# A three-sub-layer decoder block on eight cores: weight loads tied to TensorE's progress, both steps of the inverse roots on GpSimd, own-row sums placed later

## The chip, the cores and the metric

One Trainium2 chip, 8 cores. The same program runs on all eight, each on its own 2,048 rows of the sequence (2 batches of 8,192 rows, four cores to a batch); no core talks to another. The metric is the time of the slowest core in device microseconds, the median of several runs. The names of the engines in the rows: PE is TensorE (matmul), PEld its weight load, DVE VectorE, ACT ScalarE, POOL GpSimd, SP the sync engine; a q behind a name is that engine's instruction queue, which issues transfers too.

## The reference, cut to what matters

With D = 1024, D_FF = 2816 and nine modulation vectors per batch (shift, scale and gate for each of three sub-layers, from `silu(c) @ w_ada + b_ada`):

```
h = modulate(rms_norm(x), sh1, sc1);  x = x + 0.5 * gt1 * swiglu(h, ffn1)
h = modulate(rms_norm(x), sh2, sc2);  x = x + gt2 * hybrid_mixer(h)
h = modulate(rms_norm(x), sh3, sc3);  x = x + 0.5 * gt3 * swiglu(h, ffn2)
rms_norm(x)      = x / sqrt(mean(x*x) + 1e-6) * g
modulate(h,s,c)  = h * (1 + c) + s
swiglu(h)        = (silu(h @ w_gate) * (h @ w_up)) @ w_down
```

The mixer projects h to queries, keys, values and convolution inputs, runs dilated causal attention over the last 2,048 positions and a short convolution, merges both by gates and projects again. Because of the attention's reach every core also needs h of the 2,048 rows ahead of its own (its halo), and computes the first feed-forward part for them itself.

## The kernel before, in words

**Stages.** A core's 16 tiles of 128 rows are taken in four groups `tg` of 512 rows. The order of the work is: first feed-forward over the halo rows (pass 0, from `xh`), the same over the own rows (pass 1, from `xo`), the mixer, the second feed-forward over the own rows. The rows live in `xbuf` (tensor `A`, f32), the transposed and normed input of the matmuls in `hT` (tensor `B`), the weights in two slots of tensor `Dw`, hidden values in `E` (and parts of `C`).

**Feed-forward (`ffn`).** D_FF is cut into six `PIECES` of 4, 4, 2, 4, 4, 4 column blocks of 128. For each piece and each of the four row groups there is a unit: `gu` does the gate and up projections (for each block j eight matmuls into bank j%2, a Silu by ACT, eight matmuls into bank 2+j%2, a product by DVE into `hid`), and `down` the down projection (8 groups of `nj` matmuls, each followed by a DVE addition into `xbuf`). Two passes of six pieces give pieces p = 0 to 11; the second feed-forward has p = 0 to 5. Piece p uses slot p%2. The weights of piece p+2 are loaded while piece p+1 runs: `load_gu` has eight transfers (four gate, four up), `load_d` one transfer for each block, and 20 us of planned time later DVE multiplies the down weights by the gate row (`scale_task`). The transfers are issued by POOL and convert f32 to bf16.

**The plan.** The program's order is written by a planner at build time. `P.t` is a planned time that advances with every matmul (0.213 us for 512 columns). Side work is written as generators on lanes (`Lanes`); `yield x` asks to be resumed when `P.t` is x later, and `L.tick()`, called after every group of matmuls (every 1.7 planned us in `gu`, 0.85 in `down`), resumes what is due. So the plan says beside which matmul an instruction is written. At run time there is no clock: each engine works through its own queue in order, and an instruction waits only for the semaphores of what it reads, overwrites, or follows on its DMA channel. `quiet()` makes the load generators pause while `P.t < L.hold`; `head` of `Norm` sets `L.hold` 8 planned us past every norm it writes. `L.finish(task)` writes all that is left of a task at once; `ffn` calls it before the first unit of a piece (gate and up loads) and before its first `down`.

**The norms (`Norm`, `norm_pe`).** For a row group: four sums of squares on ACT (`sumsq`, into `ssb`), then `roots`: a multiply and add on DVE, `(mean + eps)`, 128 x 4 values, then a power of -0.5 on POOL; then `scaled`, four multiplications of 128 x 1024 on POOL, each followed by a DMA transpose issued by SP into the transposed buffer; after `settle` planned us the `rest`: eight DVE modulations of 128 x 512 in three portions. `norm_pe` (only in the opening) transposes on PE instead.

**Where the two passes meet.** When the last piece of pass 0 (piece 5) is through `down` for row group tg, `post(u)` starts `n2[0, tg]`, the mixer's norm of the halo rows (delay 1.5, settle 15, in buffers `xn_a` of `C`). Behind its scaling, `mid` loads the own rows of that group over the halo rows (`load_x(xo_d, tg)`, 2 MB) and starts `n1[1, tg]`, the own rows' norm for the first feed-forward, 11 planned us later and with settle 11. It must be finished before piece 6 reaches that row group, about 51 planned us behind `post`. `put` stores the halo rows' h (`h2s`, 1 MB).

```
            def mid():
                load_x(xo_d, tg)
                n1[1, tg] = Norm("n1", 11.0, tg, xn_b, 2, 0, 8)
```

**Where the second feed-forward opens.** `head3` loads piece 0 and computes the last part of the mixer's output; `spawn_n3` starts norms `n3`. `late2` is called behind `gu` of the third unit and spawns both loads of piece 1, because its slot held the mixer's `mTs` and `tab`:

```
            if i == 2 and late is not None:
                late(load)
```

The opening of the first feed-forward (`opening`) has a like place: the loads of piece 1 are spawned in the middle of the fourth unit's `gu`, behind `gates()`.

Of the kernel before, what the change touches and what calls it, by code (L numbers as in the profile page):

```python
# [11 lines left out]

EPS = 1e-6
D = 1024
KC = 8
# [256 lines left out]
def build_nc():  # L272
# [27 lines left out]
    P = Prog()  # L300
# [35 lines left out]
    def mm(out, lhsT, rhs, start, stop):  # L336
        cols_ = 1
        for _, c in list(rhs.ap)[1:]:
            cols_ *= c
        P.t += max(cols_ / 2400.0, 0.027)  # L340
        return P.op("pe", "matmul", out, lhsT=lhsT, rhs=rhs, start=start, stop=stop)

# [22 lines left out]

    def wide_load(dst, src, chan):
        return P.op("pool", "dma_start", out=dst, in_=src.rearrange("(k p) n -> p k n", p=128), chan=chan)

# [7 lines left out]

    def load_gu(w, s, j0, nj):

        n = nj * 128
        for q in range(4):  # L380
            for j, nm in ((0, "wg"), (1, "wu")):
                yield from quiet()
                wide_load(SV[s][j][:, 2 * q:2 * q + 2, 0:n], w[j][q * 256:(q + 1) * 256, j0 * 128:j0 * 128 + n], (nm, s, q))
                yield 3.4

    def load_d(w, s, j0, nj):
        for j in range(nj):
            yield from quiet()
            wide_load(SV[s][2][:, j:j + 1, :], w[2][(j0 + j) * 128:(j0 + j + 1) * 128, :], ("wd", s, j))
            yield 3.4  # L390
# [93 lines left out]
    def roots(tg, ss):  # L484
        c0 = ss * NT + 4 * tg
        ts(out=rstd[:, c0:c0 + 4], in0=ssb[:, c0:c0 + 4], scalar1=1.0 / D, scalar2=EPS, op0=ALU.mult, op1=ALU.add)
        tt("pool", out=rstd[:, c0:c0 + 4], in0=rstd[:, c0:c0 + 4], in1=mhalf[:], op=ALU.pow)
# [16 lines left out]
    class Norm:  # L504
# [7 lines left out]
        def head(self, lane, tg, xns, ss, acol, scol, mid, post, dst, hurry, settle, before):  # L512
# [8 lines left out]
            roots(tg, ss)  # L521
            L.hold = max(L.hold, P.t + 8.0)
            for i in range(4):
# [82 lines left out]
    def ffn(passes, pre, post, head=None, flip=0, gates=None, each=None, late=None):  # L606
# [12 lines left out]
        def load(p, what):  # L619
# [4 lines left out]
            if what == 0:  # L624
                ups[p] = L.spawn("up", load_gu(w, s, j0, nj))
                if p == 0:
                    L.finish(ups[p])
            else:
                now = load_d(w, s, j0, nj)
                if p == 0:  # L630
# [74 lines left out]
    P.op("pool", "dma_start", out=brow, in_=bada_d[2 * D:3 * D].rearrange("(o n) -> o n", o=1), chan="brow")  # L705
    run(load_d(f1, 0, *PIECES[0]))
    n1[0, 0] = None
# [27 lines left out]
    def post(u):  # L735
        tg = u.tg
        tk = slice(tg * 512, (tg + 1) * 512)
        if u.pi == 0:
# [4 lines left out]
            def mid():  # L743
                load_x(xo_d, tg)
                n1[1, tg] = Norm("n1", 11.0, tg, xn_b, 2, 0, 8)

# [496 lines left out]
```

How the kernel before makes its waits and increments, by code:

```python
                def body(engine, ops_e=ops_e, e=e):  # L207
                    for op in ops_e:
                        for k, v in op.waits:
                            engine.wait_ge(sems[k], v)
                        if op.fn is None:
                            continue
                        name, a, kw = op.fn
                        ins = getattr(engine, name)(*a, **kw)
                        if op.chan is not None:
                            ins.then_inc(sems[("c", op.chan)], 16)
                        elif op.needs_inc:
                            ins.then_inc(sems[("e", e)], 1)
```

## Time and profile before

| | us |
|---|---|
| median of 3 runs, slowest core | 2414.03 (2408.94 to 2418.44) |
| the profiled execution, its own time | 2409.29 |
| span of its slowest core (core 3) | 2407.7 |
| PE busy in that span | 2270.4 (94%) |
| DVE, ACT, POOL busy | 1098.9, 609.0, 513.8 |
| spans of the eight cores | 2389.7 to 2407.7 |

The profile is of one execution and one core. Its time is 1.6 us more than the span of the core. Every instruction stands under the line of the helper that issues it (L214), so instructions are told apart by their tiles: `C<-A` with 128x1024 elements on ACT is a sum of squares, `rstd` the roots, `C<-A,rstd` the scaling, `B<-C` or `C<-C` on SP a transpose, `B<-B,cols` a modulation, `E<-ps,E` the product of gate and up, `A<-ps,A` the addition behind a down projection, `Dw<-ffn_w_...` a weight load. The figure in brackets at the end of a timeline row is the engine's idle time ahead of the instruction, and what ended it.

### The profile page before, as it was taken

How to read it: one execution, taken by the hardware profiler on the slowest of the kernel's cores; microseconds unless marked ns; L12 is line 12 of the kernel's file. 1: busy time of each engine (PE TensorE's matmuls, PEld its weight loads, DVE VectorE, ACT ScalarE, POOL GpSimd, SP SyncE). 2: the span in 40 equal slices, each digit the busy share in tenths (PEclk: the TensorE clock that was granted, in tenths of full speed). 3: DMA queues.
4: the chain of work that ended last, by engine and by line, in shares of the span. 5: the costliest groups of instructions: out<-in, count | busy, mean ns of one | idle time of the engine just before them, and what ended most of it. 6: DMA issues, size and time to landing. Idle time of an engine off the chain costs nothing.

```text
span 2407.7 us, 32141 instructions; the slowest of 8 cores (2389.7 to 2407.7 us)
## 1 busy us (share of the span) xinstructions
PE 2270.4 (94%) x11524; PEld 1051.0 (44%) x11524; DVE 1098.9 (46%) x1876; ACT 609.0 (25%) x1044; POOL 513.8 (21%) x612
## 2 busy tenths in 40 slices
PE   3999999987999999989999999999999979999999
PEld 1444444433444444434444544444444434434444
DVE  1264544455534444454444444666434434454444
ACT  2501111132010111245676665211122211111110
POOL 2300201134201220133544535210011221020100
PEclk8999999999999999999999999999999989999999
DMA  9932713359536651474242535831111442150302
GB/s 184 169 47 36 100 23 53 53 145 205 85 48 87 88 93 48 101 145 59 33 47 37 56 40 78 117 37 26 49 48 49 105 80 27 14 83 10 53 36 105
DMA packets 260586, 174.48 MB, mean 72 GB/s; under 512 B 172112, under 2 KB 239824, under 8 KB 258512
## 3 DMA queue, kind: packets, MB, share of 16 engines
q0 software_dynamic: 152336, 135.82, 34.9%
q1 hardware_dynamic: 108096, 36.62, 8.0%
q8 instruction: 96, 1.57, 0.3%
q14 instruction: 58, 0.48, 0.1%
HBM read 221.56 MB, written 20.97 MB: 101 GB/s over the span
## 4 chain that ended last, share of the span: by engine, by line
PE 84%; DMA 6%; ACT 2%; issue 2%; DVE 2%; POOL 2%; SPq 1%; another core or an unknown queue 0%; DVEq 0%; ACTq 0%; POOLq 0%
PE ps L214 84%; DMA Dw<-ffn_w_gate 2%; DMA C<-C 1%; SPq L214 1%; ACT Dw L214 1%; ACT C L214 1%; DMA A<-xo 1%; POOL C L214 1%; DMA B<-C 1%; DVE A L214 1%; DMA B<-B 1%; DMA B<-Dw 0%; POOL rstd L214 0%; ACT A L214 0%; DMA A<-Dw 0%
## 5 line engine op out<-in xcount | busy, mean ns | idle before, releaser
L214 PE MATMUL ps<-B,Dw 128*128 128x512 bf16 x6144 | 1391.8, 384 | 40.5 <-DVE E L214 20.2
L214 PEld LDWEIGHTS ps<-B,Dw 128*128 128x128 bf16 x6144 | 600.7, 99 | 759.1 <-issue 83.4
L214 DVE TENSOR_TENSOR A<-ps,A 128x512 f32<-128x512 f32 (+2 forms) x768 | 480.5, 644 | 184.1 <-PE ps L214 177.4
L214 ACT ACTIVATE E<-ps 128x512 f32<-128x512 f32 x296 | 176.2, 596 | 1316.6 <-PE ps L214 1276.3
L214 PE MATMUL ps<-Dw,E 128*128 128x512 bf16 x2048 | 467.8, 380 | 29.1 <-DVE A L214 27.1
L214 DVE TENSOR_TENSOR E<-ps,E 128x512 bf16<-128x512 f32 (+1 forms) x288 | 199.0, 691 | 649.1 <-PE ps L214 642.0
L214 PEld LDWEIGHTS ps<-Dw,E 128*128 128x128 bf16 x2048 | 195.4, 98 | 285.0 <-issue 62.4
L214 ACT ACTIVATE Dw<-ps 128x512 bf16<-128x512 f32 (+2 forms) x280 | 163.3, 588 | 259.9 <-PE ps L214 256.7
L214 POOL DMA_DIRECT2D Dw<-ffn_w_gate x70 | 51.6, 737 | 451.6 <-PE ps L214 451.6
L214 POOL TENSOR_TENSOR Dw<-Dw,E 128x512 bf16<-128x512 bf16 x96 | 110.7, 1153 | 142.9 <-ACT Dw L214 142.7
L214 PE MATMUL ps<-B,C 128*128 128x512 bf16 x512 | 121.0, 379 | 0.0
L214 DVE CAST Dw<-ps 128x512 bf16<-128x512 f32 x72 | 48.1, 668 | 136.2 <-PE ps L214 131.8
L214 ACT ACTIVATE Dw<-ps,cols 128x512 f32<-128x512 f32 x120 | 80.7, 673 | 60.9 <-PE ps L214 60.3
L214 PE MATMUL ps<-A,Dw 128*128 128x512 bf16 x384 | 93.3, 379 | 0.0
L214 POOL DMA_DIRECT2D Dw<-w_in x60 | 55.3, 929 | 173.1 <-PE ps L214 163.2
L214 PE MATMUL ps<-C,Dw 128*128 128x512 bf16 (+1 forms) x384 | 81.1, 357 | 5.7 <-DVE Dw L214 5.7
L214 DVE SCALAR_TENSOR_TENSOR Dw<-Dw,ps 128x512 f32<-128x512 f32 x64 | 43.9, 687 | 92.9 <-PE ps L214 87.4
L214 PE MATMUL ps<-Dw,A 128*128 128x128 bf16 x768 | 72.0, 221 | 13.1 <-DVE A L214 10.7
L214 PEld LDWEIGHTS ps<-Dw,A 128*128 128x128 bf16 x768 | 56.7, 98 | 47.6 <-issue 25.3
L214 ACT ACTIVATE Dw<-Dw 128x512 f32<-128x512 f32 x120 | 74.3, 619 | 11.3 <-ACT Dw L214 0.4
L214 PE MATMUL ps<-Dw,ones_s 128*128 128x512 bf16 (+1 forms) x216 | 72.3, 335 | 5.0 <-ACT Dw L214 5.0
L214 PEld LDWEIGHTS ps<-B,C 128*128 128x128 bf16 x512 | 50.1, 98 | 60.4
(88 smaller groups left out, 1086.8 us busy)
## 6 DMA issues: line engine op xcount, KB each, us to landing
Dw<-ffn_w_down POOLq DMA_DIRECT2D x66, 256.0 KB, 10.5
Dw<-w_in POOLq DMA_DIRECT2D x60, 256.0 KB, 5.8
Dw<-ffn_w_gate POOLq DMA_DIRECT2D x56, 256.0 KB, 8.6
Dw<-ffn_w_up POOLq DMA_DIRECT2D x56, 256.0 KB, 10.5
C<-w_ada POOLq DMA_DIRECT2D x24, 512.0 KB, 8.1
A<-xo POOLq DMA_DIRECT2D x4, 2048.0 KB, 11.3
x1s<-A POOLq DMA_DIRECT2D x4, 2048.0 KB, 7.2
A<-x1s POOLq DMA_DIRECT2D x4, 2048.0 KB, 8.7
```

Of the source, the lines that this page charges most:

```text
L214: ins = getattr(engine, name)(*a, **kw)
```

## The change

Four edits. Every `wide_load` of `load_gu` and `load_d` with `paced` true gets `P.last`, the matmul written last at that point of the plan, as a further dependence: POOL's queue then waits for that matmul's semaphore before it issues the load. `paced` is true for p > 0, so for 16 of the 18 pieces. `HOLD` is 14 where 8 stood. The first step of `roots` moves from DVE to POOL, where the second is. The own rows' norm starts 20 planned us behind `mid` where 11 stood, and its modulations follow its roots after 16 where 11 stood.

```diff
--- before.py
+++ after.py
@@ -11,6 +11,7 @@
 ALU = mybir.AluOpType
 
 EPS = 1e-6
+HOLD = 14.0
 D = 1024
 KC = 8
 DFF = 2816
@@ -338,7 +339,8 @@
         for _, c in list(rhs.ap)[1:]:
             cols_ *= c
         P.t += max(cols_ / 2400.0, 0.027)
-        return P.op("pe", "matmul", out, lhsT=lhsT, rhs=rhs, start=start, stop=stop)
+        P.last = P.op("pe", "matmul", out, lhsT=lhsT, rhs=rhs, start=start, stop=stop)
+        return P.last
 
     def turn(out, in_, chan):
         return P.op("sp", "dma_start_transpose", out=out, in_=in_, chan=chan)
@@ -363,8 +365,8 @@
     def load_x(src_d, tg):
         P.op("pool", "dma_start", out=xbuf[:, 4 * tg:4 * tg + 4, :], in_=src_d[:, 4 * tg:4 * tg + 4, :], chan=("xg", tg))
 
-    def wide_load(dst, src, chan):
-        return P.op("pool", "dma_start", out=dst, in_=src.rearrange("(k p) n -> p k n", p=128), chan=chan)
+    def wide_load(dst, src, chan, after=()):
+        return P.op("pool", "dma_start", out=dst, in_=src.rearrange("(k p) n -> p k n", p=128), chan=chan, after=after)
 
     slots = [Dw[:, s * 12288:(s + 1) * 12288] for s in range(2)]
 
@@ -374,19 +376,23 @@
                 b[:, 8192:12288].rearrange("p (j n) -> p j n", j=4))
     SV = [slot_views(s) for s in range(2)]
 
-    def load_gu(w, s, j0, nj):
+    def here(paced):
+
+        return (P.last,) if paced else ()
+
+    def load_gu(w, s, j0, nj, paced=True):
 
         n = nj * 128
         for q in range(4):
             for j, nm in ((0, "wg"), (1, "wu")):
                 yield from quiet()
-                wide_load(SV[s][j][:, 2 * q:2 * q + 2, 0:n], w[j][q * 256:(q + 1) * 256, j0 * 128:j0 * 128 + n], (nm, s, q))
+                wide_load(SV[s][j][:, 2 * q:2 * q + 2, 0:n], w[j][q * 256:(q + 1) * 256, j0 * 128:j0 * 128 + n], (nm, s, q), here(paced))
                 yield 3.4
 
-    def load_d(w, s, j0, nj):
+    def load_d(w, s, j0, nj, paced=True):
         for j in range(nj):
             yield from quiet()
-            wide_load(SV[s][2][:, j:j + 1, :], w[2][(j0 + j) * 128:(j0 + j + 1) * 128, :], ("wd", s, j))
+            wide_load(SV[s][2][:, j:j + 1, :], w[2][(j0 + j) * 128:(j0 + j + 1) * 128, :], ("wd", s, j), here(paced))
             yield 3.4
 
     def run(gen):
@@ -483,7 +489,7 @@
 
     def roots(tg, ss):
         c0 = ss * NT + 4 * tg
-        ts(out=rstd[:, c0:c0 + 4], in0=ssb[:, c0:c0 + 4], scalar1=1.0 / D, scalar2=EPS, op0=ALU.mult, op1=ALU.add)
+        ts("pool", out=rstd[:, c0:c0 + 4], in0=ssb[:, c0:c0 + 4], scalar1=1.0 / D, scalar2=EPS, op0=ALU.mult, op1=ALU.add)
         tt("pool", out=rstd[:, c0:c0 + 4], in0=rstd[:, c0:c0 + 4], in1=mhalf[:], op=ALU.pow)
 
     def scaled(tg, xns, ss, i, other):
@@ -519,7 +525,7 @@
             if before is not None:
                 before()
             roots(tg, ss)
-            L.hold = max(L.hold, P.t + 8.0)
+            L.hold = max(L.hold, P.t + HOLD)
             for i in range(4):
                 scaled(tg, xns, ss, i, "dve" if hurry else "pool")
                 for ap, k0, k1 in xns[i].parts:
@@ -622,11 +628,11 @@
             pi, q, w, gi, j0, nj = seq[p]
             s = (p + flip) % 2
             if what == 0:
-                ups[p] = L.spawn("up", load_gu(w, s, j0, nj))
+                ups[p] = L.spawn("up", load_gu(w, s, j0, nj, p > 0))
                 if p == 0:
                     L.finish(ups[p])
             else:
-                now = load_d(w, s, j0, nj)
+                now = load_d(w, s, j0, nj, p > 0)
                 if p == 0:
                     run(now)
 
@@ -703,7 +709,7 @@
     load_x(xh_d, 3)
     wide_load(blk[2], wada_d[:, 2 * D:3 * D], "blk2")
     P.op("pool", "dma_start", out=brow, in_=bada_d[2 * D:3 * D].rearrange("(o n) -> o n", o=1), chan="brow")
-    run(load_d(f1, 0, *PIECES[0]))
+    run(load_d(f1, 0, *PIECES[0], False))
     n1[0, 0] = None
     n1[0, 1] = L.spawn("n1", norm_pe(1, xn_b, 0, 0, 8), 6.5)
     n1[0, 2] = L.spawn("n1", norm_pe(2, xn_b, 0, 0, 8))
@@ -742,7 +748,7 @@
 
             def mid():
                 load_x(xo_d, tg)
-                n1[1, tg] = Norm("n1", 11.0, tg, xn_b, 2, 0, 8)
+                n1[1, tg] = Norm("n1", 20.0, tg, xn_b, 2, 0, 8, settle=16.0)
 
             def put(m):
                 P.op("pool", "dma_start", out=h2s_d[:, :, tk], in_=hss[tg % 2], chan=("h2s", tg))
```

## Rows read from the trace of the kernel before

**Rows 1.** The page: the span, and which core it is.
```profile
span 2407.7 us, 32141 instructions; the slowest of 8 cores (2389.7 to 2407.7 us)
```

**Rows 2.** What PE waited for, whole span: total us, times, longest.
```profile
PE ps L214 <- DVE A L214: 37.8, 23, 16.6
...
PE ps L214 <- DVE E L214: 20.9, 7, 5.7
...
PE ps L214 <- ACT E L214: 7.8, 4, 2.4
```

**Rows 3.** Two stretches: us; busy PE, PEld, DVE, ACT, POOL; clock; DMA share; GB/s.
```profile
490.20:610.60 120.40, 92.79 (x386) 38.91 (x385) 69.24 (x121) 38.15 (x72) 52.85 (x56) 0.90 0.82 184
1939.10:1978.50 39.40, 22.81 (x97) 9.78 (x96) 10.65 (x20) 2.39 (x4) 3.54 (x6) 0.78 0.61 97
```

**Rows 4.** Timeline, PE, two starts of `down` that nothing disturbs.
```profile
1978.54 7.07 PE L214 MATMUL ps<-Dw,E 128*128 128x512 bf16 x32
...
1999.26 7.07 PE L214 MATMUL ps<-Dw,E 128*128 128x512 bf16 x32
```

**Rows 5.** Timeline, where the passes meet: load, sums, and PE's two pauses.
```profile
476.67 0.69 DVE L214 TENSOR_TENSOR A<-ps,A 128x512 f32<-128x512 f32 x1 [0.17 <-PE ps L214]
...
489.74 0.62 POOL L214 DMA_DIRECT2D A<-xo  x1 [0.58 <-POOL C L214]
...
501.68 1.06 ACT L214 ACTIVATE C<-A 128x1024 bf16<-128x1024 f32 x1 [12.28 <-DMA A<-xo]
...
506.56 1.89 PE L214 MATMUL ps<-B,Dw 128*128 128x512 bf16 x8 [2.38 <-ACT E L214]
...
507.36 5.23 DVE L214 TENSOR_SCALAR C<-C,cols 128x512 bf16<-128x512 bf16 x6
...
513.33 6.88 PE L214 MATMUL ps<-B,Dw 128*128 128x512 bf16 x19 [4.88 <-DVE E L214]
```

**Rows 6.** What DVE waited for from 478 to 604 us.
```profile
DVE rstd L214 <- ACT C L214: 35.9, 5, 8.8
```

**Rows 7.** Transfers, us to landing: transposes at 486, 491, 522, 1944; own rows.
```profile
C<-C SPq DMA_TRANSPOSE x1, 3.3
...
C<-C SPq DMA_TRANSPOSE x1, 12.3
...
C<-C SPq DMA_TRANSPOSE x1, 13.9
...
B<-C SPq DMA_TRANSPOSE x1, 17.2
...
A<-xo POOLq DMA_DIRECT2D x1, 2048.0 KB, 11.8
```

**Rows 8.** Timeline of 1930 to 1962: transposes, first and last of twelve loads, PE's pause.
```profile
1934.90 18.93 SPq L214 DMA_TRANSPOSE B<-C  x4
...
1934.64 0.78 POOL L214 DMA_DIRECT2D Dw<-ffn_w_gate  x1
...
1941.85 0.79 POOL L214 DMA_DIRECT2D Dw<-ffn_w_up  x1
...
1961.88 1.87 PE L214 MATMUL ps<-Dw,E 128*128 128x512 bf16 x4 [16.59 <-DVE A L214]
```

**Rows 9.** Weight transfers, us to landing: near-alone at 734.5, 736.3; burst from 275.
```profile
Dw<-ffn_w_gate POOLq DMA_DIRECT2D x1, 256.0 KB, 3.9
...
Dw<-ffn_w_up POOLq DMA_DIRECT2D x1, 256.0 KB, 4.6
...
Dw<-ffn_w_gate POOLq DMA_DIRECT2D x4, 256.0 KB, 11.5
```

**Rows 10.** The tile `rstd`: ns min/median/max, first and last start.
```profile
L214 DVE TENSOR_SCALAR rstd<-ssb x20: 157/170/172, 17.3 to 1928.7; 128x4 f32<-128x4 f32 x20
L214 POOL TENSOR_TENSOR rstd<-rstd,mhalf x20: 1006/1032/1377, 17.6 to 1929.0; 128x4 f32<-128x4 f32 x20
```

**Rows 11.** Timeline, DVE: modulations with POOL not scaling beside them.
```profile
1033.05 1.05 DVE L214 TENSOR_SCALAR B<-B,cols 128x512 bf16<-128x512 bf16 x3
```

## The prediction, made before the changed kernel had run

> **What bounds the kernel now.** I read the page first, then PE's waits, then a table of stretches, then the timeline of the two worst. The span is 2407.7 us [rows 1] and PE computes in 94% of it, so what can be had is PE's idle time and its time at half clock. Three groups of waits matter, on the halves of work that DVE and ACT hand back: 37.8, 20.9 and 7.8 us [rows 2]. The table of stretches says where most of it lies [rows 3]. From 490.2 to 610.6, where halo pass and own pass meet, PE is busy for 92.79 of 120.40 us and its mean granted clock is 0.90. From 1939.1 to 1978.5, at the opening of the second feed-forward, it is busy for 22.81 of 39.40 us at 0.78. An undisturbed unit of four blocks takes 1999.26 - 1978.54 = 20.72 us [rows 4]. The first stretch is four units, 82.9 us, so its excess is 37.5 us: 27.6 idle, and 9.9 in which PE ran at 1.2 instead of 2.4 GHz after its pauses. The second is one unit and has 18.7 us too much: 16.6 idle and 2.1 of slow clock. Together 56.2 us: all that this change aims at.
>
> **Why PE pauses there.** In the first stretch the own rows' load is issued at 489.74 and takes 11.8 us [rows 5, 7]. The sums that need it are written about 9 planned us earlier than it lands, so ACT stands for 12.28 us until 501.68, with Silus behind the sums; PE pauses for 2.38 us for a Silu. DVE has the first step of the roots in its queue and stands with ACT: 35.9 us in five waits [rows 6]. When it is free it owes six modulations (5.23 us), and PE waits another 4.88 us for the product behind them [rows 5]. The pattern comes four times. The second stretch is a collision. Four transposes stand in SP's queue from 1934.90; POOL, whose slot is free, issues twelve weight loads from 1934.64 to 1941.85 although the plan writes them some 55 us into the stage, behind the third unit's gate and up work; the last transpose takes 17.2 us where an unhindered one takes 3.3, DVE waits for it, and PE stands for 16.59 us [rows 7, 8].
>
> **Part 1, the wait on the matmul.** In the second stretch it moves all twelve loads behind the third unit's gate and up work. The transposes then meet no weight traffic: issued to about 1940, landed 3.3 us later, with the modulations due at about 1942. I book 17.5 of the 18.7 us, about 1 us being left for a transpose a little late. What queues behind a waiting load is POOL's later work; it is written later in the plan too and mostly hangs on PE's results of that moment, so I cost that at nothing. It is covered as long as POOL has slack (513.8 us busy of 2407.7).
>
> What becomes late is the end of each piece's loads. Eight gate and up loads at 3.4 planned us need 27 us; a normal piece has 82 from their spawning to its first unit, the two-block piece some 44, and a weight load lands in 3.9 to 4.6 us with little beside it [rows 9]. So the steady pieces lose nothing. Two places have little slack. In the opening, spawning and first use are 27.3 planned us apart: the last gate load goes out 5.1 us and the last up load 1.7 us before the unit, whose matmuls ask for them 1.3 and 3.0 us into it; landing fits within half a us, and I take 0. In the second feed-forward the distance is 20.5 us, six loads fit, and `finish` writes the last gate and up load with a wait on the last matmul ahead of the unit. PE does six matmuls of 0.216 us (1.3 us) and stands until the gate load lands: 0.15 to wake POOL (my estimate, from the gap of 0.17 us behind PE in [rows 5]) + 3.9 + 0.1 - 1.3 = 2.9 us. The up load lands before it is asked for. Bounds: 0, if a row is late anyway, and 11.5 - 1.3 = 10.2 us at a burst's landing [rows 9]; 2.9 is nearest, as by then only those two are in flight.
>
> **Part 2, the own rows' sums 9 us later.** Counted from `post` at 476.6, where the group's last additions run [rows 5], the load goes out at 13.1 us and lands at 25; the sums are now due at the tick of 25.6 planned, 25.9 real. ACT no longer stands, and PE's waits for Silus go. The own modulations are due at 46 behind their `post`, needed at 51, so the pass does not wait.
>
> **Part 3, the first root step on POOL.** Twenty times DVE loses 0.17 us and one hand-over; POOL gains an operation [rows 10]. POOL's only 128 x 4 row is the power, 1.03 us, which bounds it from above; below it is 0.1. It is nearer in kind to a multiply than to a power, so I take 0.3, less the hand-over saved: 0 on the path. The ends are -0.1 and +0.9 us for each of some seven places where PE hangs on the roots (three in the opening, four where the mixer opens): -1 to +6 in all. What it brings is that DVE no longer stands for ACT's sums (35.9 us in this stretch [rows 6]).
>
> **Part 4, HOLD 14.** It closes more of the meeting stretch to loads. With roots at 5.1 and 29.0 planned us behind each `post`, 20.5 apart, what stays open for piece 7's loads is one slot at 64, two at 84 to 90, and all from 104 behind the first `post`. Each lane has its last gate or up load out by 118, for a `finish` at 133. No cost; the transposes there meet one or two loads in place of six.
>
> **What is late next in the meeting stretch.** The fourth transpose of the halo norm is issued just behind the own rows' load and takes 12.3 us, and 13.9 with the store of h beside it [rows 7]. Nothing in the change moves that. It lands at 25.8 (first group) or 27.3 behind `post`, while the modulations are due at 20.7. DVE then does six (2.1 us at 0.35 [rows 11]) and the product (0.69): 28.6 or 30.1, against 29.4 when PE wants that bank. Then come eight own modulations before the next unit may end its first group, about 1.6 us late in all. So about 0 + 3 x 1.6 = 5 us stay, and 2 us for half clock behind them: 37.5 - 7 = 30 us gained. If the modulations went at 0.87 us (six in 5.23 [rows 5]), 14 of them would add 7 us to each of three groups, 21 in all.
>
> Here a rule bears on the rows. A transpose took 3.3 us alone and 12.3 behind a load of 2 MB, so I let it wait for the load. The Trainium skill, DMA: Bandwidth & Descriptors, section Queues, rings and completion order, has it that each DMA engine goes round-robin over the queue rows it has work for, one packet at a time, so that SP's transpose would share with POOL's load and not stand behind it. By that rule the sum would be that of the clean rival below; the rows do not agree with it in size.
>
> **The sum.** -30 (meeting) - 17.5 (opening of the second feed-forward) + 2.9 (late pair) + 0 (roots) = -44.6. On the profiled execution's 2409.3 us that gives 2364.7, on the median of 2414.0, which is 4.7 higher, 2369.4. I forecast 2368.
>
> **The rivals.** *Both stretches clean.* If transposes shared the engines fairly with the load beside them, the fourth would take about twice 3.3 us, land at 20, and nothing would stay of the 37.5 and 18.7: -56.2 + 2.9 = -53.3, 2361 us. Against it: 12.3 and 17.2 us are four and five times 3.3 [rows 7]; for it: at 1940 the twelve loads that the change moves away are all there is beside the transposes. This is where the skill's round-robin rule would lead. Chance 0.20.
>
> *The meeting stretch stays bad.* The late transpose and 16 modulations in a row keep DVE behind, at 0.87 us each: 21 us more than booked, so only 9 us are gained there: -9 - 17.5 + 2.9 = -23.6, 2390 us. For it: the fourth transpose there takes 13.9 us today [rows 7]. Against: POOL scales at another time. Chance 0.19.
>
> *Loads late at every piece: slower.* If the 16 paced pieces had no slack, through a hold or a wait of POOL's queue behind something slow, each would end like the late pair. At 2.9 us each, 46 us, that eats the gain; beyond it the change loses. With the eight loads out together at 11.5 us, less 1.3, it is 10.2 x 16 = 163 us: 2414 - 47 + 163 = 2530. Against it stand 82 us of distance for 27 us of issue. Chance 0.05.
>
> *The wait binds nowhere*, because the slots free at the planned time anyway: then the collision at 1940 stays and only parts 2 and 3 count, about half of the first stretch's 27.6 idle us: 2400. The twelve loads in 7.2 us, against 20.5 planned [rows 8], say otherwise. Chance 0.04.
>
> **How the numbers follow.** My case has 0.52. Range 2353 to 2392: the low end is the clean case with 8 us for chip and run, the high end the bad meeting stretch; outside lie slower, not binding and the tails. A measurement of this kernel can tell about 0.5% (12 us) from no change. Faster by more: 0.52 + 0.20 + 0.19, less a little, 0.90; within: 0.05; slower: 0.05.
>
> **What the profile of after would show.** Right: the twelve loads of piece 1 of the second feed-forward 3.4 us apart behind the third unit, the pause of 16.59 us gone, one of about 3 us before the fifth unit, waiting for a `ffn_w_gate` or `ffn_w_up` load; DVE with no wait for the sums; ACT's wait for `A<-xo` near 0; PE's clock at 1.00 around 600; the stretch of four units near 90 us in place of 120.4. Wrong: pauses of PE for weight loads in several pieces; product waits of 3 us or more in the meeting stretch (then DVE's C<-C waits are the cause); POOL's step above 1 us.

## The result, and the profile after

The changed kernel took 2396.25 us, the median of five runs, beside 2410.51 for the kernel before, the median of five too. The ratio is 0.9927, with a 95% interval of 0.9907 to 0.9948, and is taken from the means of the executions, 2394.8 and 2412.4 us. (Executions in which the cores of one die ran at a much lower granted clock than the other's, such as those of 2610.8 and 2708.5 us among the five, are left out of it and of every ratio and mean below.) So the kernel is faster by 0.73%, 14 us by the medians and 17.5 by these means, and not by the 45 that were forecast; 2396.25 lies above the range of 2353 to 2392.

The page, and the waits of PE over the whole span, for core 4, the slowest of the profiled execution. They answer to [rows 1] and [rows 2]; the columns of a wait are total us, times, longest.

```profile
span 2391.3 us, 32217 instructions; the slowest of 8 cores (2364.4 to 2391.3 us)
```

```profile
PE ps L215 <- DVE A L215: 21.0, 23, 3.3
PE ps L215 <- DVE E L215: 16.5, 5, 12.2
...
PE ps L215 <- DMA Dw<-ffn_w_gate: 8.5, 3, 4.4
PE ps L215 <- DVE B L215: 7.7, 6, 5.8
```

PE's wait for additions (`DVE A`) fell from 37.8 to 21.0 us and its longest from 16.6 to 3.3: the pause at the opening of the second feed-forward is gone. The waits for Silus (`ACT E`, 7.8 before) have left the list. But the product wait (`DVE E`) now has a single piece of 12.2 us where the longest was 5.7, and `DVE B`, the wait for the modulations of the own rows, is new.

Two measures carry the rest. **By units:** on every core I read the starts of `down` from PE's timeline and take the distance from one to the next, which is 20.7 us undisturbed [rows 4]. The meeting stretch is the eight units around the meeting, 165.8 us undisturbed; the four of them that the prediction spoke of are the third to the sixth. The opening of the second feed-forward is taken as its first four units, 82.9 us undisturbed. Means over the eight cores of one profiled execution:

| unit of the meeting stretch | 1st, 2nd | 3rd | 4th | 5th | 6th | 7th, 8th | all eight | opening of 2nd FF |
|---|---|---|---|---|---|---|---|---|
| before | 20.7 | 29.0 | 28.0 | 31.4 | 30.0 | 20.7 | 201.2 | 99.7 |
| after | 20.7 | 20.7 | 28.2 | 22.6 | 34.6 | 20.7 | 189.0 | 90.5 |

So 12.2 us came from the meeting stretch and 9.2 from the opening of the second feed-forward. The time up to the first of these marks grew from 448.1 to 450.7 us, and what lies between the two places changed by -1.0. The sum is -19.8, and so is the difference of the mean spans of the eight cores (2399.8 and 2380.0). The metric takes the slowest core of each execution, and that one gained less, 16.4 us here (2407.7 to 2391.3).

**By middle core:** for the small differences between experiments I take the median of the eight spans of a timed execution, its mean over the executions, and its distance from the same number of the kernel before on the same chip. Its standard error is 1 to 4 us (e9 and e10 have a single execution each, so none). The stretches, by contrast, are read from one profiled execution of each kernel.

The table of stretches for core 4: the four units of the meeting, a part of them, then the third unit of the second feed-forward. The first row answers to the first of [rows 3]; columns as there.

```profile
493.30:607.90 114.60, 92.12 (x386) 38.58 (x385) 59.68 (x108) 38.36 (x72) 50.50 (x56) 0.87 0.87 186
...
565.00:601.50 36.50, 18.52 (x79) 7.67 (x76) 9.75 (x21) 5.46 (x9) 9.36 (x12) 0.75 1.06 190
1977.10:2003.90 26.80, 22.43 (x98) 9.68 (x97) 8.30 (x12) 2.39 (x4) 7.70 (x12) 0.94 0.83 120
```

On this core the four units still take 114.6 us: 22.5 idle, and, against 82.9, another 9.2 at the lower clock. Of the idle time, 18.0 us are in the 36.5 us from 565.0, where PE is busy for 18.5 and the busy share of the DMA engines is 1.06, beside 0.87 for the four units.

What DVE and ACT waited for from 470 to 640 us, core 4. This answers to [rows 6].

```profile
DVE C L215 <- DMA C<-C: 30.3, 4, 17.2
DVE B L215 <- DMA B<-C: 10.2, 3, 8.2
...
ACT C L215 <- DMA B<-C: 20.1, 3, 16.3
```

DVE's wait for sums (35.9 us before) is gone, and ACT no longer waits for `A<-xo`. Both now wait for transposes: DVE for those of the halo rows (`C<-C`) and of the own rows (`B<-C`), ACT for transposes that still read the buffers into which the next own-row sums write.

The timeline of core 4 at the fourth row group, chosen lines. It answers to [rows 5].

```profile
563.68 0.62 POOL L215 DMA_DIRECT2D A<-xo  x1 [0.58 <-POOL C L215]
564.30 0.93 POOL L215 DMA_DIRECT2D h2s<-C  x1
...
572.66 23.34 SPq L215 DMA_TRANSPOSE B<-C  x4
...
575.29 0.78 POOL L215 DMA_DIRECT2D Dw<-ffn_w_up  x1 [4.01 <-PE ps L215]
...
579.43 0.56 POOL L215 DMA_DIRECT2D Dw<-ffn_w_down  x1
...
589.30 2.03 DVE L215 TENSOR_SCALAR C<-C,cols 128x512 bf16<-128x512 bf16 x6 [17.23 <-DMA C<-C]
...
592.08 3.57 PE L215 MATMUL ps<-B,Dw 128*128 128x512 bf16 x8 [12.17 <-DVE E L215]
...
593.49 1.06 ACT L215 ACTIVATE C<-A 128x1024 bf16<-128x1024 f32 x1 [16.34 <-DMA B<-C]
...
600.79 1.06 DVE L215 TENSOR_SCALAR B<-B,cols 128x512 bf16<-128x512 bf16 x3 [8.21 <-DMA B<-C]
...
601.46 2.04 PE L215 MATMUL ps<-B,Dw 128*128 128x512 bf16 x4 [5.81 <-DVE B L215]
```

Own rows, store of h and four weight loads are issued within 16 us. DVE stands for 17.23 us in front of the halo norm's modulations, with PE's product queued behind them, and PE loses 12.17 us. The six modulations then take 2.03 us. Next the own rows' modulations are late too, for 5.81 us more. The transfers of that moment, us from issue to landing: the fourth halo transpose, issued at 565.30, the first own transpose, issued at 572.66, and for comparison three of the first group (490 to 492). They answer to [rows 7]:

```profile
C<-C SPq DMA_TRANSPOSE x1, 23.7
...
B<-C SPq DMA_TRANSPOSE x1, 20.7
...
C<-C SPq DMA_TRANSPOSE x3, 3.2
```

Core 4 is one of two cores on which the long pause stands in front of the product. The mean over the eight cores is 6.0 us of waits for the product (`DVE E`; single pieces above 10 us only on cores 3 and 4) and 10.2 us for the own modulations (`DVE B`; 11.0 to 12.9 us at once on cores 1, 2, 5 and 6).

Even the issue of a transpose stood still. In the chain of waits of the same core, SP's queue holds two single pieces of 7.21 and 11.54 us, the issues of these same two transposes, where an undisturbed one has 1.23:

```profile
559.93 1.23 SPq L215
...
565.30 7.21 SPq L215
...
572.66 11.54 SPq L215
```

At the opening of the second feed-forward, core 4 (timeline; answers to [rows 8]):

```profile
1976.11 0.79 POOL L215 DMA_DIRECT2D Dw<-ffn_w_gate  x1 [44.93 <-PE ps L215]
...
1979.56 0.71 POOL L215 DMA_DIRECT2D Dw<-ffn_w_up  x1 [2.10 <-PE ps L215]
...
1995.10 0.72 POOL L215 DMA_DIRECT2D Dw<-ffn_w_gate  x1 [0.99 <-PE ps L215]
1995.82 0.72 POOL L215 DMA_DIRECT2D Dw<-ffn_w_up  x1
...
2000.20 2.29 PE L215 MATMUL ps<-B,Dw 128*128 128x512 bf16 x5 [4.37 <-DMA Dw<-ffn_w_gate]
```

The twelve loads start at 1976.11, behind the matmuls they are tied to: the gate and up loads 3.45 us apart, with the four down loads beside the first four of them. Before, all twelve stood within 7.2 us, beside the transposes. The last gate and up load go out together at 1995.10 and 1995.82, and PE waits 4.37 us for the first of them.

The step that moved to POOL (answers to [rows 10]; ns min/median/max):

```profile
L215 POOL TENSOR_SCALAR rstd<-ssb x20: 189/196/484, 17.7 to 1925.2; 128x4 f32<-128x4 f32 x20
```

### The profile page after: what moved, and what is told of

Its sections match the earlier page's. It is cut to its first block, busy times and chain, and to the rows that moved or that the text cites. A ratio compares the mean times of both kernels' runs of the same rounds, so it can differ in the third digit from the quotient of the medians.

```text
span 2391.3 us, 32217 instructions; the slowest of 8 cores (2364.4 to 2391.3 us)
## 1 busy us (share of the span) xinstructions
PE 2268.7 (95%) x11524; PEld 1049.9 (44%) x11524; DVE 1089.2 (46%) x1856; ACT 609.2 (25%) x1044; POOL 518.5 (22%) x632
## 4 chain that ended last, share of the span: by engine, by line
PE 86%; DMA 4%; SPq 2%; ACT 2%; issue 2%; POOL 2%; DVE 1%; another core or an unknown queue 0%; DVEq 0%; ACTq 0%; POOLq 0%
PE ps L215 86%; SPq L215 2%; DMA Dw<-ffn_w_up 2%; ACT Dw L215 1%; DMA B<-C 1%; POOL C L215 1%; DVE A L215 1%; ACT C L215 1%; DMA B<-Dw 1%; POOL rstd L215 0%; ACT A L215 0%; DMA A<-Dw 0%; POOL Dw L215 0%; DVE Dw L215 0%; DMA Dw<-ffn_w_gate 0%
## 5 line engine op out<-in xcount | busy, mean ns | idle before, releaser
L215 POOL DMA_DIRECT2D Dw<-ffn_w_up x70 | 50.4, 719 | 162.1 <-PE ps L215 161.9
L215 PE MATMUL ps<-Dw,A 128*128 128x128 bf16 x768 | 72.0, 221 | 13.1 <-DVE A L215 12.3
L215 ACT ACTIVATE Dw<-Dw 128x512 f32<-128x512 f32 x120 | 74.3, 619 | 11.6 <-ACT Dw L215 0.8
## 6 DMA issues: line engine op xcount, KB each, us to landing
A<-xo POOLq DMA_DIRECT2D x4, 2048.0 KB, 11.3
```

What stands on the lines that cost most here:

```text
L215: ins = getattr(engine, name)(*a, **kw)
```

## The experiments

Each is the changed kernel with the edit shown, unless it says otherwise. In the first expectations "six units" and "a unit less" go by the marks as I counted them then; measured is always the eight-unit stretch defined above.

### Which part did what

**e1: the own rows' norm back to its old place.**

```diff
-                n1[1, tg] = Norm("n1", 20.0, tg, xn_b, 2, 0, 8, settle=16.0)
+                n1[1, tg] = Norm("n1", 11.0, tg, xn_b, 2, 0, 8)
```

> The changed kernel with the own rows' norm back at 11 planned us behind the load and a settle of 11; wait, hold of 14 and roots on POOL stay. Over the eight cores the meeting stretch (six units, from the second down of piece 4's last unit on) took a mean of 201.2 us before and 189.0 changed; undisturbed it is 165.8 less a unit. Theory A (the later own norm put its four transposes behind the next group's 2 MB load and store, where SP, ACT and DVE stand in turn, and that costs most of what did not come): the waits of ACT for a transpose B<-C and the double digit pauses of PE go, the early wait for the own rows' load comes back at about 12 us of ACT per group but costs PE only some 2 us each, and the stretch gets shorter than 189, the kernel 5 to 10 us faster than the change. Theory B (the later norm is what brought the gain in that stretch): it goes back towards 201 and the kernel to about 2400 to 2405.

Measured: ratio 0.9936 (0.9892 to 0.998); meeting stretch 198.9, middle core -12.4 us. The waits of core 4, 470 to 650 us:

```profile
PE ps L215 <- DVE A L215: 21.5, 4, 9.3
...
ACT C L215 <- DMA A<-xo: 61.0, 4, 17.0
```

ACT stands for the own rows again, up to 17.0 us at a time. The later place is worth some 10 us of the stretch (198.9 beside 189.0), and 7 by the middle core (-12.4 beside the -19.5 of e13 below).

**e4: the wait alone** (HOLD 8, roots on DVE, own norm early).

```diff
-HOLD = 14.0
+HOLD = 8.0
-        ts("pool", out=rstd[:, c0:c0 + 4], in0=ssb[:, c0:c0 + 4], ...
+        ts(out=rstd[:, c0:c0 + 4], in0=ssb[:, c0:c0 + 4], ...
-                n1[1, tg] = Norm("n1", 20.0, tg, xn_b, 2, 0, 8, settle=16.0)
+                n1[1, tg] = Norm("n1", 11.0, tg, xn_b, 2, 0, 8)
```

> The kernel before with the wait on the matmul alone: hold of 8, roots as before, own norm as before. The wait by itself should remove the pause of 16.6 us at the opening of the second feed-forward and bring the pause for the late pair (5 to 6 us on each core of the changed kernel, with 2 us of slow clock): the five downs there 91.4 us in place of 101.6. If that is all it does, about -10 us, 2400, and the meeting stretch stays at 201 us. If spacing the weight loads also helps the meeting stretch, that gets shorter by up to 5 us; if the wait harms it (loads now pushed into the transposes of the last groups), it gets longer.

Measured: ratio 0.9944 (0.99 to 0.9988), middle core -10.9 us. Cores 4 to 7 of its profile give 201.3 for the meeting stretch, as before the change, and 90.3 for the opening of the second feed-forward. The wait does its work at the second place and none at the first.

**e5: all but the wait.**

```diff
     def here(paced):
-        return (P.last,) if paced else ()
+        return ()
```

> The changed kernel without the wait on the matmul; hold 14, roots on POOL and later own norm stay. The pause at the opening of the second feed-forward comes back (16 us, five downs about 100 us in place of 90.4) and the pause for the late pair goes. In the meeting stretch theory W says POOL runs ahead of the hold only where its queue is free: piece 7's loads stand behind roots that wait for ACT, so they go out at about the planned time anyway and the stretch stays near 189; if the wait matters there, it is above 195. Kernel about 2405.

Measured: ratio 0.9978 (0.9941 to 1.0014), middle core -6.3 us. The meeting stretch is 188.9, as with the wait. The opening of the second feed-forward is 97.0, with cores from 87.4 to 104.7; on core 6 the old pause is there (waits, 1880 to 2050 us):

```profile
PE ps L215 <- DVE A L215: 19.0, 1, 19.0
...
DVE B L215 <- DMA B<-C: 19.0, 1, 19.0
```

The two halves of the change add up within the error: -10.9 for the wait and -6.3 for the rest make -17.2, where e13 below has -19.5 for both.

**e2: HOLD back to 8.**

```diff
-HOLD = 14.0
+HOLD = 8.0
```

> The changed kernel with a hold of 8 in place of 14. Theory W (weight loads beside the transposes cost the fourth group's pause): more of piece 7's loads now go out between the norms, so the meeting stretch is longer than 189, about 195 to 200, the kernel about 2403. My booking in the prediction (the hold costs and gains nothing): 189 and 2396.

Measured: ratio 0.9956 (0.9913 to 0.9999), meeting stretch 202.2, middle core -11.8. The worst core, 0, from 470 to 660 us:

```profile
PE ps L215 <- DVE B L215: 33.4, 4, 31.9
...
DVE B L215 <- DMA B<-C: 34.3, 2, 33.2
```

With HOLD at 8 the fifth unit takes 36.5 us on average (22.6 with 14) and the whole gain of the later norm is lost. HOLD 14, which I had booked at nothing, is thus worth 13 us of the stretch (8 by the middle core) once the own norm is late. Each alone is worth next to nothing. Beside the wait alone (-10.9), the later norm with HOLD at 8 has -11.8 (e2), and HOLD 14 with the early norm has -12.4 (e1).

**e3 and e14: the first root step back on DVE**, on two chips.

```diff
-        ts("pool", out=rstd[:, c0:c0 + 4], in0=ssb[:, c0:c0 + 4], ...
+        ts(out=rstd[:, c0:c0 + 4], in0=ssb[:, c0:c0 + 4], ...
```

> The changed kernel with the first step of the roots back on DVE. With the own sums written later, ACT seldom stands, so DVE's root step should wait little. If the move to POOL still matters, DVE's waits for ACT's sums come back with more than 5 us in the meeting stretch and it grows by 3 us or more; if the later sums alone did it, the stretch stays at 189 +- 2.

> e3 once more (first root step back on DVE). If POOL's root step costs time where the passes meet (POOL's queue then stands at the sums with the transfers behind it, or one more POOL instruction shifts the loads against the transposes), the stretch is again near 182 and under that of e13 by 5 us or more. If it was luck, the two are within 3 us.

Measured: 0.9935 (0.989 to 0.9979) and 0.9922 (0.9881 to 0.9963); middle core -21.8 and -22.9; meeting stretch 182.4 and 195.2. The 12.8 us between two profiled executions of one kernel are a warning about single profiles, and so about every stretch here that rests on one. The timed runs say that the step's engine makes no difference that shows; if any, DVE is the better by 2 or 3 us.

**e13: the changed kernel once more**, on the chip and beside the runs of e14 and e15, no edit.

> The changed kernel as it is, once more, on the chip of the next two. The meeting stretch was 189.0 us in its first execution and 190.2 in e7, which is the same there. If that is its level, 187 to 192 again, with a pause of 10 us or more on half of the cores; if the 182.5 of e3 was the luck of one execution, this can come out at 183 too.

Measured: 0.9937 (0.9909 to 0.9964), middle core -19.5, meeting stretch 187.7.

### What keeps the meeting stretch long

**e8: no weight loads there.** The gate, up and down loads of piece 7 wait until the last own norm is through.

```diff
+        def behind_norms(gen):
+            while not ((1, 3) in n1 and n1[1, 3].main.done):
+                yield 1.0
+            yield from gen
...
-                ups[p] = L.spawn("up", load_gu(w, s, j0, nj, p > 0))
+                gen = load_gu(w, s, j0, nj, p > 0)
+                if gates is not None and p == 7:
+                    gen = behind_norms(gen)
+                ups[p] = L.spawn("up", gen)
...
+                if gates is not None and p == 7:
+                    now = behind_norms(now)
```

> The changed kernel, with the eight gate and up loads and the four down loads of piece 7 held back until the last own norm's roots are written, so no weight load goes out while the passes meet. The meeting stretch is now read as eight units, from the down of piece 4's second to last unit to that of piece 6's last, 165.8 us undisturbed, 201.2 before, 189.0 changed (mean of eight cores). Theory W (the eight loads let in at 64 and at 84 to 90 planned us stretch the fourth group's transposes to 20 us and more): the double digit pause of the fourth group goes on all cores, the stretch falls to about 176. Theory X (the 2 MB load and the 1 MB store do it): no more than 3 us of difference, and one core or another still has a pause above 10 us.

Measured: ratio 0.9896 (0.9832 to 0.9961), middle core -30.5 us (-19.5 for the changed kernel in e13), meeting stretch 180.6. The sixth unit fell from 34.6 to 23.5 us; the fourth stayed at 27.7. The waits of core 2, the worst in the stretch:

```profile
PE ps L215 <- DVE E L215: 5.2, 1, 5.2
...
DVE C L215 <- DMA C<-C: 23.7, 4, 10.7
```

On core 4 the fourth halo transpose still takes 18.8 us to land (23.7 with the weight loads), but the first own transpose 11.3 (20.7), and PE's waits for the own modulations fall from 10.2 to 1.9 us for a core. So weight loads like the four at 575 to 579 are what makes pauses of 12 us out of shorter ones. The bill at the other end is 1.4 us in the eighth unit (22.1 us); that the loads now come close to their use there is my reading, not shown by a row.

**e9: a quarter of the own rows.** Only one of each group's four tiles is loaded, 0.5 MB in place of 2, so the rest of the own rows is not computed from its input.

```diff
-                load_x(xo_d, tg)
+                P.op("pool", "dma_start", out=xbuf[:, 4 * tg:4 * tg + 1, :], in_=xo_d[:, 4 * tg:4 * tg + 1, :], chan=("xg", tg))
```

> The changed kernel with only the first of the four tiles of each group's own rows loaded (0.5 MB in place of 2; the other three groups of rows keep what the halo pass left, so three quarters of the own rows are not the reference's). Theory X: the fourth transpose of each halo norm lands in about 5 us in place of 12 to 14, DVE's waits for C<-C (19.6 us a core) and B<-C (11.6 us) fall under 5 us each, the meeting stretch to about 170 to 174 us. Theory W: both waits stay in the fourth group, the stretch stays above 182.

In its single execution the meeting stretch is 172.5 us; the fourth unit is down to 23.1 and the sixth to 21.7, weight loads and all. DVE, core 2:

```profile
DVE C L215 <- DMA C<-C: 0.9, 2, 0.5
```

The own rows' load is the larger part of it: without three quarters of its bytes, neither the store of h nor the weight loads do much harm. Its middle core is -38.5 us.

**e6: the own rows' load 4.5 planned us later,** so that the fourth transpose of the halo norm goes first.

```diff
-                load_x(xo_d, tg)
+                def later():
+                    load_x(xo_d, tg)
+                    yield 0.0
+                L.spawn("xo", later(), 4.5)
```

> The changed kernel, with the own rows' load written 4.5 planned us later, so that on POOL it comes behind the previous group's own norm and all eight transposes of a group are issued before it. Theory A (transposes standing behind the 2 MB load and the 1 MB store are the cause): DVE's waits for C<-C and B<-C (17.2 and 8.2 us at worst on one core) and SP's issues of 7 to 11 us mostly go; what comes is a wait of ACT for the own rows' load of about 5 us per group, with little slack, 1 to 2 us of PE each; meeting stretch about 178 to 183 us, kernel about 8 us faster than the change. Rival (the weight loads let in at 64 and 84 planned us are the cause): no difference, the worst pause of PE stays in the fourth group.

Measured: ratio 0.9892 (0.9825 to 0.996), but middle core -19.3, like the changed kernel; meeting stretch 194.7. DVE's waits for the halo transposes went from 19.6 us for a core to 4.2, and those for the own transposes from 11.6 to 33.8. Core 6, 470 to 660 us:

```profile
PE ps L215 <- DVE B L215: 41.6, 3, 22.4
...
DVE B L215 <- DMA B<-C: 55.3, 3, 27.0
```

The wait moved from one norm to the other.

**e10: the own rows in four tiles,** 4 planned us apart, each with a wait on a matmul.

```diff
-                load_x(xo_d, tg)
+                def tiles():
+                    for i in range(4):
+                        n = 4 * tg + i
+                        P.op("pool", "dma_start", out=xbuf[:, n:n + 1, :], in_=xo_d[:, n:n + 1, :], chan=("xo", i), after=(P.last,))
+                        yield 4.0
+                L.spawn("xo", tiles())
```

> The changed kernel, with each group's own rows loaded by four transfers of 512 KB, 4 planned us apart and each with a wait on the matmul beside it, in place of one of 2 MB. The same bytes, spread over 12 us more. Theory X: a transpose now finds at most one tile ahead of it, some 3 us, so it lands in 4 to 8 us; DVE's waits for transposes fall by half or more, the stretch to about 176 to 180, the kernel about 8 us faster than the change; the sums find their tiles in time (last tile out at 12, landed by 17, due at 20). If it is the number of bytes in the stretch that counts and not how they are bunched, nothing changes (within 3 us).

A single execution, so no ratio. Meeting stretch 192.6; a single unit took up to 52 us, and DVE's waits for own transposes were 24.9 us for a core (11.6 in the changed kernel). Spreading a transfer over the transposes is no better than having it in one piece; the gain of 8 us that I expected is not there.

### The late pair, and both repairs

**e7: the loads of piece 1 of the second feed-forward spawned one unit earlier.**

```diff
-            if i == 2 and late is not None:
+            if i == 1 and late is not None:
```

> The changed kernel, with the loads of piece 1 of the second feed-forward spawned one unit earlier (behind the second unit's gate and up work in place of the third's). All eight gate and up loads are then out 27 planned us later with some 14 to spare, and they still start 10 us or more after the last transposes. The pause of 4.4 to 5.9 us for a ffn_w_gate load and the 2 us of slow clock behind it go: five downs take 83 to 85 us in place of 91.4, the kernel about 7 us faster than the change. If the pause is only replaced by another wait of DVE for transposes, it is no faster.

Measured: ratio 0.9881 (0.9804 to 0.9958), middle core -23.6; the four units took 83.4 us, 0.5 above undisturbed. The late pair has time, and the transposes, which stand close before, don't suffer. On core 3 one wait of PE is left from 1880 to 2050 us; the longest on any core is 3.6 us (core 7), and none is for a weight load:

```profile
PE ps L215 <- DVE A L215: 0.8, 1, 0.8
```

**e11: e7, e8 and e10 together.**

> The three repairs together: own rows in tiles, no weight load while the passes meet, the loads of the second feed-forward's piece 1 one unit earlier. If X and W both hold a part, the meeting stretch is 168 to 174 us and the five downs of the second feed-forward 83.4: 15 to 20 + 7 us less than the changed kernel, about 2370. If neither does, 2388.

Measured: 0.991 (0.9875 to 0.9944), middle core -28.9, meeting stretch 188.1. The tiles give back what e8 gained (180.6 there; -36.8 in e12, the same without the tiles).

**e12: e7 and e8 together; e15: the same with the root step on DVE.**

> The changed kernel with piece 7's loads held back until the last own norm (as in e8) and the loads of the second feed-forward's piece 1 one unit earlier (as in e7). The two repairs sit in different stretches, so their gains add: meeting stretch 180.6 and five downs 83.4, 15.5 us less than the changed kernel, about 2380, a ratio to the kernel before of 0.986 to 0.988. If the earlier loads or the held-back ones meet something else, one of the two numbers moves back by itself.

> e12 (piece 7's loads held back, piece 1's of the second feed-forward one unit earlier) with the first root step on DVE. If that step on POOL costs by itself, the meeting stretch falls from 180.2 to about 174 and this is the fastest of all; if it only decided how the weight loads met the transposes, there are none left to meet and it stays at 179 to 182.

Measured: 0.9869 (0.9791 to 0.9947) and 0.9888 (0.9816 to 0.996); meeting stretch 180.2 and 181.9; opening of the second feed-forward 83.2 and 83.1. The middle core is 36.8 and 35.5 us below that of the kernel before, some 16 below that of the changed kernel, as the stretches say (8.8 + 7.3). By the slowest core the two intervals still overlap with the changed kernel's, for a reason that the table of stretches of e12 shows, core 5 first, then core 7, each from 120 to 240 us:

```profile
120.00:180.00 60.00, 58.92 (x274) 26.61 (x273) 36.81 (x56) 4.18 (x7) 16.53 (x24) 1.00 0.64 77
180.00:240.00 60.00, 60.00 (x308) 27.59 (x306) 23.95 (x37) 7.16 (x12) 3.16 (x4) 1.00 0.36 43
...
120.00:180.00 60.00, 60.00 (x245) 26.01 (x244) 31.50 (x48) 2.99 (x5) 11.53 (x17) 0.81 0.46 62
180.00:240.00 60.00, 60.00 (x239) 25.24 (x238) 21.56 (x32) 5.97 (x10) 5.01 (x7) 0.84 0.30 36
```

Core 7 is never idle here, yet has a granted clock of 0.81; so has core 6, and both reach the meeting some 23 us late. Three of e12's five timings had this, at 2388.8 to 2394.6 us; the two without it took 2369.7 and 2371.7.

| kernel | ratio, 95% interval | middle core, us | meeting stretch | opening of 2nd FF |
|---|---|---|---|---|
| before | 1 | 0 | 201.2 | 99.7 |
| changed | 0.9927 (0.9907 to 0.9948) | -19.5 (e13) | 189.0 | 90.5 |
| e4, wait alone | 0.9944 (0.99 to 0.9988) | -10.9 | 201.3 | 90.3 |
| e5, all but the wait | 0.9978 (0.9941 to 1.0014) | -6.3 | 188.9 | 97.0 |
| e2, HOLD 8 | 0.9956 (0.9913 to 0.9999) | -11.8 | 202.2 | 90.9 |
| e8, no weights there | 0.9896 (0.9832 to 0.9961) | -30.5 | 180.6 | 90.2 |
| e7, pair earlier | 0.9881 (0.9804 to 0.9958) | -23.6 | 190.2 | 83.4 |
| e12, both | 0.9869 (0.9791 to 0.9947) | -36.8 | 180.2 | 83.2 |

## Why the prediction was wrong

**The meeting stretch, -30 booked, -12 measured: this step failed.** Of the 35.4 us that a core had there above undisturbed (201.2 - 165.8), 23.2 are still there; I had left 7. The direction of the mechanism was right. The later sums took ACT and DVE out of the wait for the own rows (35.9 us to nothing), the roots no longer held DVE, and I named what would be late next, the fourth transpose of the halo norm. The sum kept 5 us of waits and 2 of half clock; a core has 16.2 us of waits there (6.0 for the product, 10.2 for the own modulations) and, by subtraction, 7.0 of lower clock. What failed is the landing time of the transposes, in "It lands at 25.8 (first group) or 27.3 behind `post`". I carried 12.3 and 13.9 us [rows 7] over from the kernel before to all groups. On core 4 it holds for the first (12.5 us); in the fourth, with the own rows, the store of h and four weight loads within 16 us, it took 23.7, and the one issued behind it, the first of the own rows, 20.7. By units, the sixth has 13.9 us above undisturbed on average (34.6 - 20.7), the fourth 7.5 and the fifth 1.9; my 7 us were for all of them.

**HOLD 14, "No cost; the transposes there meet one or two loads in place of six": wrong twice.** It was not nothing: e2 puts it at 13 us of gain, as the later norm lives from the quiet that it makes. And the few loads that it still lets through were not harmless: e8 puts them at 8 us. I had said what stays open ("one slot at 64, two at 84 to 90") and not asked what stands in SP's queue at 84 to 90: the transposes of the fourth group.

**The pass does not wait** for the own modulations: wrong, and the larger half of the waits. With sums at 25.9 and roots at 29, their transposes are issued into the same traffic. PE's wait for them took 10.2 us for a core, up to 12.9 at once; the sum had it at nothing. Without weight loads there (e8) it is 1.9.

**Opening of the second feed-forward, -17.5 + 2.9 booked, -9.2 measured.** The first term holds: the third unit no longer begins behind a pause, and the first two take 20.8 and 20.7 us. The mis-sized term is the late pair. I took the landing of a near-lone load, 3.9 us [rows 9]; PE waited 4.4 on core 4 and up to 5.9 on others, and half clock behind the pause, which I left out, brings the unit to 28.0 us on average, 7.2 above undisturbed and not 2.9. e7, which took the pair away, gives back 7.1.

**The opening of the first feed-forward, 0:** about right. The time up to the meeting is 2.6 us longer than before, and between 0.3 and 2.9 longer in most of the other kernels, 1.2 in e5, which has no wait. Where that comes from I have not shown.

**Roots on POOL, 0:** right. The step takes 0.196 us (I had said 0.3, between 0.1 and 1.03), and neither e3 nor e14 shows an effect clear of the error.

**The slowest core.** The sum was made for core 3, the slowest, and its stretches were near the mean. The new waits are unequal instead: the sixth unit runs from 20.7 us (core 7) to 43.7 (core 4). So the mean gain of 19.8 us shrinks to 16.4 on the slowest core of the profiled executions. Those 3 us are a part of the miss which no term of mine had.

**The rivals.** "The meeting stretch stays bad" came nearest with 2390, and for a reason that did not occur: not 16 modulations at 0.87 us (six took 2.03), but transposes that land later still.

**"Both stretches clean", and what sharing means.** This rival, and the working, took "share" for equal parts of the time, so that the fourth transpose would land in about twice its time alone; the rows have 23.7 us against 3.2. The packet counts of the kernel before settle how the queues share (core 3; queue: packets, MB, share of 16 engines' time; q0 carries POOL's transfers, q1 the transposes). First from 1944 to 1954 us, with the twelve weight loads; then from 494 to 497, with the own rows' load; then transposes alone, from 489 to 491:

```profile
q0 software_dynamic: 1379, 1.63, 92.5%
q1 hardware_dynamic: 1379, 0.34, 25.9%
...
q0 software_dynamic: 50, 0.82, 96.0%
q1 hardware_dynamic: 49, 0.01, 1.8%
...
q1 hardware_dynamic: 1558, 0.39, 103.9%
```

The queues take turns, one packet each: 1379 and 1379, 50 and 49. But a packet of a transpose has about 256 B, one of a weight load 1.2 KB and one of the own rows 16 KB. Beside the own rows the transpose gets 49 packets through in 3 us, where alone there were 1558 in 2 us. So it shares, and still lands only when the load is nearly through. The fourth group of the changed kernel has the same turns, 207 and 201 packets from 574 to 580 us on core 4. This agrees with the round-robin rule of the Trainium skill (DMA: Bandwidth & Descriptors, section Queues, rings and completion order), turns between the queue rows packet by packet; what failed is the step from equal turns to equal times. That the bytes beside the transpose count, e9 shows.

Not settled: how much the store of h has in this (never moved alone), and why, in the fourth group on core 4, the first 16 packets of the own rows took 7.2 us each (359.1% of the 16 engines' time from 566 to 568 us), where the first 17 of [rows 5]'s load took 1.5. SP's issue of 7.21 us falls into the same time, before any weight load was out.

## What to carry to other kernels

A prefetch that is tied to the compute engine's progress goes where the plan has it. That is worth having wherever a slot comes free early. The price is at the end of the burst, so leave the last pair a unit of slack. When a wait is removed, ask not only what is late next but what will be in flight at that moment, group by group: transfers that the old waits had spread out can meet. And a quiet time for latency-bound transfers must cover all of them, own rows and weights, or those that are let in cost more than their number suggests. To estimate a small transfer beside a large one, compare the sizes of their packets and not only their bytes.

## What the runs showed of the hardware that I had not expected

- A DMA transpose of 3.2 us took 23.7 us beside a 2 MB load, a 1 MB store and four loads of 256 KB, and its issue by SP was itself blocked for 7.2 and 11.5 us.
- Transposes and loads take turns by the packet (1379 and 1379 packets in 10 us), whatever the packets' size: 256 B of a transpose for 1.2 KB of weights or 16 KB of own rows.
- Four loads of 512 KB, 4 planned us apart, held the transposes up no less than one of 2 MB (e10: DVE's waits for own transposes 24.9 us against 11.6, in one profiled execution of each; the stretches, 192.6 against 187.7 to 189.0, differ by less than two profiles of one kernel did).
- In the profiled executions of e3, e6 and e12, cores 6 and 7 reached the meeting some 23 us late; in e3 and e12 the table of stretches has core 7 at a granted clock of 0.80 to 0.84 from 60 to 240 us, with PE never idle from 120 on, while core 5 of the same die has 1.00 from 120 to 240 (e12). In e12 that is some 20 us on the slowest core, more than the whole change. What brings it about is not shown.
